# A split up projection with the high weights against both token parts in one 512-column matmul

## The reference, cut to what matters

```python
hid = causal_dwconv(rms_norm(h, ffn_norm_g) @ w_ffn_up, ffn_conv_w, ffn_conv_b)   # width 3
g_ff, up = jnp.split(hid, 2, axis=-1)                                              # 2816 columns each
return h + (jax.nn.silu(g_ff) * up) @ w_ffn_down
```

## Time and profile before

| | us |
|---|---|
| median of 3 runs | 719.83 |
| lowest, highest | 719.82, 720.54 |
| the profiled execution | 719.74 |
| its span in the trace | 718.0 |

### The profile page before, as it was taken

One profiled execution on the slowest core, in us unless ns is written; L12 is line 12 of the kernel. 1 busy time (PEld: TensorE's weight loads), 2 busy tenths in 40 slices (PEclk: granted clock), 3 DMA queues, 4 the chain that ended last, 5 costly groups with the idle time before them and its releaser, 6 DMA issues.

```text
span 718.0 us, 13927 instructions
## 1 busy us (share of the span) xinstructions
PE 692.0 (96%) x5478; PEld 674.3 (94%) x5478; DVE 494.1 (69%) x629; ACT 373.0 (52%) x471; POOL 9.7 (1%) x23
## 2 busy tenths in 40 slices
PE   5798989999999999999999999999999999999996
PEld 4798989999989999999999999999999999999995
DVE  4893798879776565667754445656569777777785
ACT  5543786767663445544443333444456544555552
POOL 0000000000010000000000000000000000000001
PEclk9998999999999999999999999999999999999998
DMA  8729784848635535245545755656525555555531
GB/s 257 216 60 318 223 259 133 257 131 279 219 118 176 168 126 166 96 148 175 175 139 162 243 188 175 190 192 205 175 98 197 180 193 197 190 175 175 180 114 58
DMA packets 118172, 127.94 MB, mean 178 GB/s; under 512 B 4302, under 2 KB 113279, under 8 KB 117631
## 3 DMA queue, kind: packets, MB, share of 16 engines
q1 hardware_dynamic: 118143, 127.54, 55.4%
HBM read 126.43 MB, written 2.67 MB: 180 GB/s over the span
## 4 chain that ended last, share of the span: by engine, by line
PE 83%; DVE 7%; DMA 2%; issue 2%; SPq 2%; ACT 2%; POOL 0%; DVEq 0%; POOLq 0%; ACTq 0%
PE ps L343 26%; PE ps L344 26%; PE ps L345 26%; DMA w_raw<-w_in 2%; DVE w_lo L315 2%; DVE conv_a L1244 2%; PE ps L636 1%; ACT decay L941 1%; SPq L289 1%; PE ps L655 0%; PE ps L671 0%; PE ps L621 0%; PE ps L664 0%; DVE conv_o L1251 0%; PE ps L637 0%
## 5 line engine op out<-in xcount | busy, mean ns | idle before, releaser
L343 PE MATMUL ps<-tok_hi,w_hi 128*128 128x256 f32 x1056 | 302.7, 287 | 5.1 <-DVE w_lo L315 3.3
L344 PE MATMUL ps<-tok_lo,w_hi 128*128 128x256 f32 x1056 | 300.0, 284 | 0.0
L345 PE MATMUL ps<-tok_hi,w_lo 128*128 128x256 f32 x1056 | 299.9, 284 | 0.0
L315 DVE TENSOR_TENSOR w_lo<-w_raw,w_hi 128x2048 fp32r<-128x2048 f32 x108 | 247.0, 2288 | 73.6 <-ACT w_hi L311 73.4
L311 ACT ACTIVATE w_hi<-w_raw 128x2048 fp32r<-128x2048 f32 x108 | 206.0, 1909 | 59.2 <-PE ps L345 43.4
L343 PEld LDWEIGHTS ps<-tok_hi,w_hi 128*128 128x128 f32 x1056 | 203.8, 193 | 7.5 <-DVE w_lo L315 3.5
L344 PEld LDWEIGHTS ps<-tok_lo,w_hi 128*128 128x128 f32 x1056 | 204.0, 193 | 0.4
L345 PEld LDWEIGHTS ps<-tok_hi,w_lo 128*128 128x128 f32 x1056 | 203.8, 193 | 0.0
L343 PE MATMUL ps<-os_hi,w_hi 128*128 128x256 f32 x128 | 36.3, 284 | 0.0
L345 PE MATMUL ps<-os_hi,w_lo 128*128 128x256 f32 x128 | 36.2, 283 | 0.0
L344 PE MATMUL ps<-os_lo,w_hi 128*128 128x256 f32 x128 | 36.2, 283 | 0.0
(11 more groups left out here) (282 smaller groups left out, 1167.3 us busy)
## 6 DMA issues: line engine op xcount, KB each, us to landing
w_raw<-w_in SPq DMA_DIRECT2D x95, 512.0 KB, 4.8
w_raw<-w_ffn_up SPq DMA_DIRECT2D x44, 512.0 KB, 4.4
w_raw<-w_ffn_down SPq DMA_DIRECT2D x22, 512.0 KB, 3.9
w_raw<-w_mem_kv SPq DMA_DIRECT2D x16, 512.0 KB, 4.0
w_raw<-w_br_ssm SPq DMA_DIRECT2D x16, 512.0 KB, 4.3
acs_b<-acs_d SPq DMA_DIRECT2D x4, 1024.0 KB, 7.3
w_raw<-w_br_attn SPq DMA_DIRECT2D x8, 512.0 KB, 4.4
w_raw<-w_br_mem SPq DMA_DIRECT2D x8, 512.0 KB, 4.0
```

The lines of the kernel that those rows point to most:

```text
L315: dve.tensor_tensor(w_lo[:, s, :], w_raw[:, s, :], w_hi[:, s, :].bitcast(F32), ALU.subtract).then_inc(lo_ready[s], 1)
L343: pe.matmul(o, a[0], b[0], start=start, stop=False, **kw)
L344: pe.matmul(o, a[0], b[1], start=False, stop=False, **kw)
L345: return pe.matmul(o, a[1], b[0], start=False, stop=stop, **kw)
```

## The change

The two token parts become one tile `tok`, with `tok_hi` and `tok_lo` as its halves. From step 1 on, gate and up gemms use `gemm_wide`: for each weight tile the high part meets both token parts in one matmul of 512 columns, which fills a whole bank (high x high in the lower half, high x low in the upper), and the low part meets `tok_hi` in 256 columns, in the upper half. So a gemm fills two banks: a pair of banks, 0 and 1 for gate, 2 and 3 for up. ScalarE copies the upper halves of the pair into the pad (`crossed`), VectorE adds the lower halves into `up_sum` (this frees the pair), waits for its own sum, and multiplies by `rstd_b` into the pad (`pad_ready`). Ahead of the loop TensorE waits for banks 1 and 2 of step 0 and for `rstd_b`, which lies in bank 3 until then. Steps 9 and 10 use the same two pairs.

```diff
@@ -102,8 +102,8 @@
     w_hi = place("w_hi", 24, [SLOTS, CHUNK], F32R)
     w_lo = place("w_lo", 48, [SLOTS, CHUNK], F32R)
 
-    tok_hi = place("tok_hi", 72, [KT, T], F32R)
-    tok_lo = place("tok_lo", 80, [KT, T], F32R)
+    tok = place("tok", 72, [2, KT, T], F32R)
+    tok_hi, tok_lo = tok[:, 0], tok[:, 1]
 
     sq = place("square_c", 88, [5 * P])
...
@@ -326,6 +328,24 @@
             mm = cols_part(pe, s, j, range(KT), o, hi, lo, k0, start, stop, None if j else tiles)
             if between is not None and j == 0:
                 between()
+        mm.then_inc(gemm_done[s], 1)
+
+    def gemm_wide(pe, r, s, pair, freed):
+
+        pe.wait_ge(lo_ready[s], r + 2)
+        pe.wait_ge(bank_free[pair], freed)
+        for j in range(2):
+            b = 2 * pair + j
+            for k in range(KT):
+                w = slice(k * CW + j * P, k * CW + (j + 1) * P)
+                if k:
+                    pe.matmul(ps[:, b, T:2 * T], w_lo[:, s, w], tok_hi[:, k, :], start=False, stop=False,
+                              skip_group_check=True)
+                mm = pe.matmul(halves(b), w_hi[:, s, w], tok[:, :, k, :], start=k == 0, stop=k == KT - 1,
+                               skip_group_check=True)
+                if k == 0:
+                    pe.matmul(ps[:, b, T:2 * T], w_lo[:, s, w], tok_hi[:, k, :], start=False, stop=False,
+                              skip_group_check=True)
         mm.then_inc(gemm_done[s], 1)
 
     def cols_part(pe, s, j, ks, o, hi, lo, k0=0, start=True, stop=True, tiles=None):
@@ -846,16 +866,18 @@
                 down_part(pe, s, 0, hi, lo)
                 down_part(pe, s, 1, hi, lo).then_inc(gemm_done[s], 1)
 
+            pe.wait_ge(bank_free[1], RF + 3)
+            pe.wait_ge(bank_free[2], RF + 3)
+            pe.wait_ge(rstd_b_ready, 1)
             with pe.Fori(1, F_STEPS - 2) as f:
                 r = f + (RG - 1)
-                gemm_cols(pe, r, 0, tok_hi, tok_lo)
-                gemm_cols(pe, r, 1, tok_hi, tok_lo)
+                gemm_wide(pe, r, 0, 0, r + 1)
+                gemm_wide(pe, r, 1, 1, r + 1)
                 down(r, 2, f, hid_hi, hid_lo)
-            gemm_cols(pe, RL - 1, 0, tok_hi, tok_lo)
-            gemm_cols(pe, RL - 1, 1, tok_hi, tok_lo)
-            pe.wait_ge(bank_free[2], RF + 3)
-            gemm_cols(pe, RL - 1, 2, tok_hi, tok_lo, free=())
-            gemm_cols(pe, RL, 0, tok_hi, tok_lo)
+            gemm_wide(pe, RL - 1, 0, 0, RL)
+            gemm_wide(pe, RL - 1, 1, 1, RL)
+            gemm_wide(pe, RL - 1, 2, 0, RL + 1)
+            gemm_wide(pe, RL, 0, 1, RL + 1)
             down(RL, 1, F_STEPS - 2, hid_hi, hid_lo)
             down(RL, 2, F_STEPS - 1, last_hi, last_lo)
             pe.wait_ge(hid_lo_s, F_STEPS)
@@ -1088,10 +1110,17 @@
             split_hi(act, RG, 0)
 
 
-            def ffn(f, sa, na, sb, nb, after_gate, after_up, last, first=False, hi=hid_hi):
-                for n, (s, freed, pad, conv, tile) in enumerate(((sa, na, pad_g, conv_g, 0),
-                                                                 (sb, nb, pad_u, conv_u, FT))):
-                    act.wait_ge(bank_free[s], freed)
+            def ffn(f, gate, up, after_gate, after_up, last, first=False, hi=hid_hi):
+                for n, (source, pad, conv, tile) in enumerate(((gate, pad_g, conv_g, 0), (up, pad_u, conv_u, FT))):
+                    b, freed = source[:2]
+                    if not first:
+                        s, done = source[2:]
+                        act.wait_ge(gemm_done[s], done)
+                        act.wait_ge(f_step, 8 * f - 4 + 4 * n)
+                        act.activation(pad[:, :, FTAPS - 1:], ps[:, 2 * b:2 * b + 2, T:2 * T],
+                                       ACT.Copy).then_inc(crossed, 1)
+                        act.wait_ge(pad_ready, 2 * f + n - 1)
+                    act.wait_ge(bank_free[b], freed)
                     if not first:
                         act.wait_ge((g_silu, hid_done)[n], f)
                     for j in range(2):
@@ -1111,12 +1140,12 @@
                 for rr, ss in last:
                     split_hi(act, rr, ss)
 
-            ffn(0, 1, RF + 3, 2, RF + 3, [(RG, 1)], [(RG, 2)], [], first=True)
+            ffn(0, (1, RF + 3), (2, RF + 3), [(RG, 1)], [(RG, 2)], [], first=True)
             with act.Fori(1, F_STEPS - 2) as f:
                 r = f + (RG - 1)
-                ffn(f, 0, r + 2, 1, r + 2, [(r + 1, 0)], [(r + 1, 1)], [(r + 1, 2)])
-            ffn(F_STEPS - 2, 0, RL + 1, 1, RL + 1, [(RL, 0)], [(RL, 1)], [], hi=last_hi)
-            ffn(F_STEPS - 1, 2, RF + 4, 0, RL + 2, [(RL, 2)], [(RL + 1, 0)], [], hi=end_hi)
+                ffn(f, (0, r + 2, 0, r + 1), (1, r + 2, 1, r + 1), [(r + 1, 0)], [(r + 1, 1)], [(r + 1, 2)])
+            ffn(F_STEPS - 2, (0, RL + 1, 0, RL), (1, RL + 1, 1, RL), [(RL, 0)], [(RL, 1)], [], hi=last_hi)
+            ffn(F_STEPS - 1, (0, RL + 2, 2, RL), (1, RL + 2, 0, RL + 1), [(RL, 2)], [(RL + 1, 0)], [], hi=end_hi)
             for n in range(2 * NT):
                 t = n // 2
                 act.wait_ge(y_added, n + 1)
@@ -1507,12 +1536,22 @@
             dve.wait_ge(pads_zero, 2)
 
 
-            def ffn(f, sa, ra, sb, rb, early, after_gate, after_up, hi=hid_hi, lo=hid_lo):
-
-                def pad_with(s, r, pad, splits):
-                    dve.wait_ge(gemm_done[s], r + 1)
-                    dve.tensor_tensor(pad[:, :, FTAPS - 1:], halves(s), rstd_b[:].unsqueeze(1).to_broadcast([P, 2, T]),
-                                      ALU.mult).then_inc(bank_free[s], 1)
+            def ffn(f, gate, up, early, after_gate, after_up, hi=hid_hi, lo=hid_lo, first=False):
+
+                def pad_with(n, pad, splits):
+                    b, freed, s, done = (gate, up)[n]
+                    dve.wait_ge(gemm_done[s], done)
+                    inner, spread = pad[:, :, FTAPS - 1:], rstd_b[:].unsqueeze(1).to_broadcast([P, 2, T])
+                    if first:
+                        dve.tensor_tensor(inner, halves(b), spread, ALU.mult).then_inc(bank_free[b], 1)
+                    else:
+                        dve.wait_ge(crossed, 2 * f + n - 1)
+                        if n:
+                            dve.wait_ge(pad_ready, 2 * f - 1)
+                        dve.tensor_tensor(up_sum[:], ps[:, 2 * b:2 * b + 2, 0:T], inner, ALU.add).then_inc(
+                            bank_free[b], 1)
+                        dve.wait_ge(bank_free[b], freed)
+                        dve.tensor_tensor(inner, up_sum[:], spread, ALU.mult).then_inc(pad_ready, 1)
                     for rr, ss in splits:
                         split_lo(dve, rr, ss)
 
@@ -1528,9 +1567,9 @@
                                                      cols_up[:, tap, bass.ds(tile + 2 * f + j, 1)], conv[:, j, :],
                                                      ALU.mult, ALU.add).then_inc(f_step, 1)
 
-                pad_with(sa, ra, pad_g, early)
+                pad_with(0, pad_g, early)
                 convolve(0, pad_g, conv_g, 0)
-                pad_with(sb, rb, pad_u, [])
+                pad_with(1, pad_u, [])
                 dve.wait_ge(g_tanh, f + 1)
                 dve.scalar_tensor_tensor(silu_g[:], tanh_g[:], 1.0, conv_g[:], ALU.add, ALU.mult).then_inc(g_silu, 1)
                 for rr, ss in after_gate:
@@ -1544,12 +1583,12 @@
                 dve.wait_ge(hid_hi_s, f + 1)
                 dve.tensor_tensor(lo[:], hid[:], hi[:].bitcast(F32), ALU.subtract).then_inc(hid_lo_s, 1)
 
-            ffn(0, 1, RF + 1, 2, RF + 1, [(RG, 0)], [(RG, 1)], [])
+            ffn(0, (1, RF + 3, 1, RF + 2), (2, RF + 3, 2, RF + 2), [(RG, 0)], [(RG, 1)], [], first=True)
             with dve.Fori(1, F_STEPS - 2) as f:
                 r = f + (RG - 1)
-                ffn(f, 0, r, 1, r, [(r, 2)], [(r + 1, 0)], [(r + 1, 1)])
-            ffn(F_STEPS - 2, 0, RL - 1, 1, RL - 1, [(RL - 1, 2)], [(RL, 0)], [(RL, 1)], last_hi, last_lo)
-            ffn(F_STEPS - 1, 2, RL - 1, 0, RL, [], [(RL, 2)], [(RL + 1, 0)], end_hi, end_lo)
+                ffn(f, (0, r + 2, 0, r + 1), (1, r + 2, 1, r + 1), [(r, 2)], [(r + 1, 0)], [(r + 1, 1)])
+            ffn(F_STEPS - 2, (0, RL + 1, 0, RL), (1, RL + 1, 1, RL), [(RL - 1, 2)], [(RL, 0)], [(RL, 1)], last_hi, last_lo)
+            ffn(F_STEPS - 1, (0, RL + 2, 2, RL), (1, RL + 2, 0, RL + 1), [], [(RL, 2)], [(RL + 1, 0)], end_hi, end_lo)
 
             def add_down(n):
```

More of the change, by code:

```diff
@@ L212, in build @@
     junk_y = place("junk_y", R + 52, [NT, D // 2])
+    up_sum = place("up_sum", R + 56, [2, T])
     rstd_b = place("rstd_b", R + 18.5, [T])
@@ L278, in build @@
         sem, ("pads_zero", "conv_begun", "f_step", "g_tanh", "g_silu", "hid_done", "hid_hi_s", "hid_lo_s"))
+    crossed, pad_ready = sem("crossed"), sem("pad_ready")
     down_done, y_added, y_gained, y_sumsq, y_var, y_rstd, y_left, y_right, y_out = map(
```

## The result

| | median, us | runs, us |
|---|---|---|
| before | 720.18 | 719.82 to 720.54 |
| after | 731.86 | 731.05 to 732.10 |

The changed kernel takes 1.016 times as long, with a 95% interval of 1.0143 to 1.0178. The profiled execution took 731.69 us, with a span of 729.9.

A forecast was written before the change was run, and what follows sets the result against it. TensorE bounds the kernel; after the change a chain through all three engines bounds the loop. 3.5 (entry and loop) + 3.5 (last steps) + 2.9 (clock) = 9.9 on 719.83 gives 729.7 us, range 725.0 to 732.0.

The forecast's parts named there:

- rival A: Whole kernel: the forecast itself, all delays and a clock drop included, 729.7 us; chance 60%.
- TensorE's part: Gate and up gemms, steps 1 to 10: 320 matmul pairs become wide ones, 0.012 us less each, 3.8 us saved.
- Rival D: Looped steps: two-piece operand or shared banks cost 0.3 to 0.5 us more a step, total 733 to 735; chance 10%.
- The circle: Loop: a chain of waits through TensorE, ScalarE and VectorE becomes the bound, 17.23 us a step against 16.98, +0.25.
- The entry: Ahead of the loop's first gate gemm: TensorE waits for banks 1 and 2, +1.44 us, paid once.
- The last steps: Steps 9 and 10: TensorE idles some 3.7 us, the down of step 9 comes 3.5 us later; bounds 2.5 to 4.5.
- The clock: Behind the wait before step 9's down: granted clock drops to half, costing 2.9 us; bounds 0 and 3.1.
- Rival B: Behind the wait before step 9's down: no drop of the clock, total 726.8 us; chance 20%.
- Rival C: Loop: TensorE stays the bound, 717.4 us, or 720.9 with the last steps' wait; chance 5% faster, 5% about the same.

The follow-up runs named there:

- second set of runs: The changed kernel run once more with nothing altered: 730.62 us, ratio 1.0138 to the kernel before.
- low part early: Changed kernel with VectorE's low-part subtraction moved from behind silu to ahead of the up sum, steps 1 to 10: 721.61 us, ratio 1.0008 to before.
- late entry: Changed kernel with TensorE's wait for bank 2 and rstd_b moved from ahead of the loop to between gate and up gemm: 730.69 us, ratio 1.0130 to before.
- copy first: Changed kernel with ScalarE's copy of the up banks moved ahead of the tanh: 722.69 us, ratio 1.0021 to before.

## Why the prediction came out right, and where it was off

The forecast of 729.7 and the mechanism (rival A) held: +9.9 was forecast, and behind the mark +10.3 was measured in three executions. The median of 731.86 lies 1.7 us above the 719.83 + 10.3 = 730.1 that this would give, and only 0.14 below the upper bound of 732.0. 0.4 of the 1.7 is in the median of before (now 720.18). The rest most likely lies ahead of the mark, where the change does nothing, as it does in the one execution of this set that was profiled; in the second set of runs, 9.9 us above its own median of before, it is not there. The 186.4 us of before rest on one profiled execution. Step by step:

- **TensorE's part** was right to the hundredth: 0.348 us a weight tile, with the two-piece operand at the price of a contiguous one. Rival D falls with it: the kernel without copies has the two-piece operand at 16.63 us a step, and the one with the low part early has copy and sum beside it at the same 16.63.
- **The circle** was right in every link and in its order, and undersized by 0.15: 17.38 to 17.40 instead of 17.23, within the stated bounds. The largest part of it is the hand-over from the end of `w_lo` to TensorE's start, 0.14 (571.53 + 2.28 to 573.95), where I had 0.05 from the earlier trace rows. From the gate gemm to ScalarE's copy it is 5.95, where I had 5.82; 0.09 of this is the first matmul's extra, which the prediction counted at the other end of the circle as 0.10, so 0.04 is new. The rest, 0.03, is the hand-overs to the up copy and behind it. The copy, sum and product took 0.63 to 0.67 and 0.73, as forecast (0.64, 0.73). Over eight steps it is 3.3 us where the prediction had about 2.1.
- **The entry**: 1.67 for 1.44. TensorE started 0.39 behind the end of `pad_u` (538.77 to 539.16), where I had 0.05, and 0.10 for the first matmul. Three semaphores and the loop's first instructions lie in it; which of them costs what was not tried apart. That it is VectorE's lateness and not the place of the wait is shown by the late entry.
- **The last steps**: 3.7 for 3.5, with TensorE idle 3.55 for 3.7. From step 9's gate gemm (678.27) the sum of step 10 came at 22.4 (22.2), the up sum at 27.8 (27.65), silu at 29.1 (29.0), the down at 32.2 (32.0).
- **The clock** dropped as forecast, but cost 1.66 instead of 2.9, and this is the term that was oversized. The price of 2.9 was that of 6.2 us at half speed in the earlier trace rows; here half speed lasted some 3.4 us (0.26 + 3 + 0.16 by the windows), and 3.4 / 2 = 1.7. A 512-column matmul came every 0.43 us there (713.31 to 713.74) instead of 0.23, so the price of a microsecond was right and its number was not. That it would drop at all was argued from two waits, 3.27 us with a drop and 2.19 without. The same trace has a third that the prediction passed over, 2.86 us ahead of 21.60 with the granted clock at 1.00 from 20 to 28, and the later runs have drops behind shorter waits (last section). So the length of a wait was a weak ground, though the drop came in all five profiled executions whose wait at this place was 3.4 to 3.6 us. In single microseconds of after:

```profile
710.00:711.00 1.00, 0.56 (x3) 0.50 (x4) 1.00 (x3) 0.42 (x1) 0.00 (x0) 1.00 0.00 0
711.00:712.00 1.00, 1.00 (x5) 0.81 (x4) 0.90 (x4) 0.00 (x0) 0.00 (x0) 0.87 0.00 0
712.00:713.00 1.00, 1.00 (x4) 0.78 (x3) 1.00 (x2) 0.29 (x1) 0.00 (x0) 0.50 0.00 0
...
715.00:716.00 1.00, 1.00 (x5) 0.82 (x4) 0.48 (x1) 0.00 (x0) 0.00 (x0) 0.92 0.00 0
```

- **What fell out of the sum**: the early part. I took the time of three runs of before, whose profiled one reached the mark at 531.60, near the lower end of the 531.48 to 533.77 that all executions span; later sets of before have medians of 720.6 to 721.1.
- **Luck**: the undersized loop (+1.2), entry and last steps (+0.4) and the oversized clock (-1.2) nearly cancel. That 9.9 comes so near to 10.3 is owed to this; the single terms were off by up to 1.2.
- **The prediction's use of the Trainium skill**: by "TensorE: Matmul & The Clock Gate" (Back-to-back issue gap) the saving would have been 2.5 ns a matmul, 0.8 us in all, where the trace had 12 ns. The section gives this formula for the isolated matmul and says that in a stream with weight loads both set the spacing, which the prediction did not say; here each matmul has a weight load of its own. The rows of after and the 16.63 us steps of the experiments bear out the trace's figure: with 0.8 us in 20 gemms a step would have stayed at 16.9.

Rival B (no drop of the clock) stayed out here, but the kernel with the copy first shows how near it was: a wait of 2.70 us at the same place and no drop. Rival C's premise, a circle under 16.6, is what two experiments made true by moving one instruction, and then the stretch behind the mark was 0.3 and 1.2 us longer than before, against C's +1.1. C had this with a last wait of 3.5 us, while the two kernels had 1.6 and 2.7.

## What to carry to other kernels

Before a change that makes one engine's part cheaper and gives others an instruction more, follow the operand that this engine waits for next through all the engines, with their program order, and count its spare time (here 1.7 us against two evacuations of 1.4 and 1.4). If the spare is used up, look first for an instruction of the late engine that can stand in front of its own waits: moving one subtraction into a wait of 1.24 us gave back all of the loop's loss. Keep a narrow form for steps without the cover that the loop has, and compare two kernels behind a mark up to which they do the same work, since what differs ahead of it is no effect of the change.

## What the runs showed of the hardware

- The granted clock need not fall in a wait; here it fell behind it. TensorE resumed at 710.44 with the clock at 1.00, and it fell late in the microsecond from 711 to 712, some 1.3 us later; in the two repeats it was 1.3 and 0.6 us. At 68 to 72 in the kernel before it had fallen before TensorE resumed (0.55 from 68 to 69, start at 68.71).
- Whether it falls is not settled by the wait's length alone: no drop after 2.70 us (copy first) or after 3.16 us at 69.28 (low part early), a drop after 2.19 us at 21.61 (after) and none after 2.86 us at 21.60 (before), and behind the wait of 2.4 us near 100 in three executions of the same kernel, there was a drop in one and none in two.
- A matmul of 512 columns whose operand is two pieces of 256 costs the same 0.23 us as a contiguous one (557.13 to 557.36; 0.228 in the earlier trace rows).
- The first matmul behind a wait costs 0.09 us more from start to start (0.32 for 0.23), and its start comes 0.14 us behind the end of the VectorE instruction that released it (0.05 at 15.61 in the earlier trace rows).
